# Deferred pieces of head norms are put in behind each filler step of an attention stage

## The reference

```python
h = rms_norm(x, g_mix)
proj = h @ w_in
qa, ka, va, qb, kb, vb, gate_a, gate_b = jnp.split(proj, cuts, axis=-1)
qa = rms_norm(qa.reshape(B, S, 16, 64), q_norm_swa)      # one norm per head of 64 columns
ka = rms_norm(ka.reshape(B, S, 2, 64), k_norm_swa)
qb = rms_norm(qb.reshape(B, S, 16, 64), q_norm_moba)
kb = rms_norm(kb.reshape(B, S, 16, 64), k_norm_moba)
y_a = swa_attention(qa, ka, va, sinks) @ w_up_swa        # window of 128 keys, 2 kv heads
y_b = moba_attention(qb, kb, vb) @ w_up_moba             # own block of 256, and 3 chosen past blocks
x = x + (sigmoid(gate_a) * y_a + sigmoid(gate_b) * y_b) @ w_out
x = x + hierarchical_moe(rms_norm(x, g_ffn), ...)
```

## Time and profile before

| | us |
|---|---|
| runs shown (median, lowest, highest) | 1942.26, 1939.7, 2071.72 (3 runs) |
| the profiled execution: its time | 1940.69 |
| the same: span of its slowest core (core 1) | 1939.1 |
| spans of the 8 cores | 1922.6 to 1939.1 |
| TensorE busy on core 1 | 1664.2 (86%) |
| ScalarE, VectorE busy | 743.0 (38%), 820.7 (42%) |

### The profile page before, as it was taken

The page is one execution under the profiler, slowest core; times in us unless marked ns, Lnnn a source line. Parts: engine busy times, 40 slices in busy tenths (PEclk is TensorE's granted clock), DMA queues, the critical chain, the costliest instruction groups (busy, mean ns, idle before and its releaser), DMA issues.

```text
span 1939.1 us, 30864 instructions; the slowest of 8 cores (1922.6 to 1939.1 us)
## 1 busy us (share of the span) xinstructions
PE 1664.2 (86%) x11342; PEld 1072.2 (55%) x11342; DVE 820.7 (42%) x1244; ACT 743.0 (38%) x1246; POOL 143.5 (7%) x283
## 2 busy tenths in 40 slices
PE   2775777889998988879999999998588899898995
PEld 1542344566566566454444444887466676666662
DVE  3634334434434443421211212233435567665765
ACT  4654446556665655671111110032331322323221
POOL 0010100200201200001111100000000000010000
PEclk9887888899999999989999999999789999999997
DMA  9469891895995999546998972851139789798796
GB/s 255 170 101 115 104 122 23 105 115 68 121 113 70 123 121 117 114 66 110 138 121 120 141 98 53 245 122 66 25 71 244 163 208 234 179 216 207 193 236 212
DMA packets 57084, 263.09 MB, mean 136 GB/s; under 512 B 10464, under 2 KB 10720, under 8 KB 49312
## 3 DMA queue, kind: packets, MB, share of 16 engines
q0 software_dynamic: 27168, 152.06, 57.7%
q1 hardware_dynamic: 29760, 108.96, 17.2%
HBM read 404.65 MB, written 73.40 MB: 247 GB/s over the span
## 4 chain that ended last, share of the span: by engine, by line
PE 72%; DVE 9%; ACT 7%; issue 5%; DMA 4%; SPq 1%; DVEq 0%; ACTq 0%
PE psum L1116 11%; PE psum L586 11%; PE psum L1529 10%; PE psum L607 6%; PE psum L1121 6%; PE psum L1304 6%; PE psum L1565 5%; PE psum L933 4%; PE psum L915 4%; DMA arena<-wbf 3%; PE psum L1551 3%; PE psum L1464 2%; DVE arena L1473 2%; DVE arena L921 1%; DVE arena L559 1%
## 5 line engine op out<-in xcount | busy, mean ns | idle before, releaser
L586 PE MATMUL psum<-arena 128*128 128x512 bf16 (+1 forms) x1072 | 286.7, 403 | 13.6 <-DVE arena L559 13.5
L1529 PE MATMUL psum<-arena 128*128 128x256 bf16 x2048 | 243.7, 273 | 5.8 <-DMA arena<-wbf 5.8
L1529 PEld LDWEIGHTS psum<-arena 128*128 128x128 bf16 x2048 | 199.8, 98 | 55.9 <-issue 8.3
L1116 PE MATMUL psum<-arena 128*128 128x512 bf16 x1024 | 226.2, 379 | 0.0
L926 ACT ACTIVATE arena<-psum 128x512 bf16<-128x512 f32 x352 | 197.9, 592 | 34.8 <-PE psum L915 33.3
L933 PE MATMUL psum<-arena 128*128 128x256 bf16 x832 | 164.6, 280 | 49.9 <-ACT arena L923 41.9
L586 PEld LDWEIGHTS psum<-arena 128*128 128x128 bf16 x1072 | 106.8, 103 | 121.1 <-issue 50.9
L1116 PEld LDWEIGHTS psum<-arena 128*128 128x128 bf16 x1024 | 100.2, 98 | 120.6
L915 PE MATMUL psum<-arena 78*128 78x256 bf16 x832 | 166.0, 281 | 0.0
L1554 DVE TENSOR_TENSOR arena<-psum,arena 128x1024 f32<-128x1024 f32 x128 | 153.8, 1221 | 10.2 <-PE psum L1551 4.0
L559 DVE SCALAR_TENSOR_TENSOR arena<-psum,arena 64x512 bf16<-64x512 f32 (+3 forms) x121 | 89.4, 739 | 144.1 <-ACT arena L556 136.6
(11 more groups left out here) (152 smaller groups left out, 1831.1 us busy)
## 6 DMA issues: line engine op xcount, KB each, us to landing
wbf<-wexp POOLq DMA_DIRECT2D x108, 512.0 KB, 36.1
arena<-wbf SPq DMA_DIRECT2D x108, 512.0 KB, 12.6
arena<-wexp POOLq DMA_DIRECT2D x84, 512.0 KB, 10.5
arena<-win POOLq DMA_DIRECT2D x58, 512.0 KB, 9.3
arena<-xs SPq DMA_DIRECT2D x24, 1024.0 KB, 8.3
arena<-wobf SPq DMA_DIRECT2D x14, 1024.0 KB, 6.0
wobf<-wo POOLq DMA_DIRECT2D x8, 1024.0 KB, 57.4
arena<-wup POOLq DMA_DIRECT2D x16, 512.0 KB, 11.8
```

The source lines that it names most:

```text
L586: prog.add("pe", lambda e, k=k: e.matmul(PS(bank, 0, n), lhsT=wslot[s][:, k, :], rhs=src[:, k, lo:lo + n], start=(k == 0), stop=(k == 15)) ...
L1116: prog.add("pe", lambda e, k=k, bank=bank, wt=wt, tl=tl: e.matmul(PS(bank), lhsT=wt[:, k, :], rhs=hTo[:, k, tl:tl + 512], start=(k == 0), ...
L1529: prog.add("pe", lambda e, k=k, f=f, bank=bank, Wv=Wv: e.matmul(PS(bank, f * 256, f * 256 + 256), lhsT=Wv[:, k, :], rhs=X[:, k, e4 * 256:( ...
```

## The change

`fill` now takes one piece out of `later` ahead of each filler step. Between two steps of four matmuls that follow each other there is thus one piece; the calls at the unit's end stay.

```diff
@@ -958,6 +958,7 @@
                 c, fns = steps[pos_[seg]]
                 pos_[seg] += 1
                 spent[seg] += c
+                pop_later()
                 for fn in fns:
                     fn()
```

## The result

The changed kernel takes 1895.21 us in the median of four runs (1892.64 to 1897.16). Against the kernel before, run beside it, the ratio is 0.9763, with a 95% interval of 0.9736 to 0.9791: faster by more than 2%, by some 46 us. A second set of six runs gave 0.9731.

The account below looks back on a forecast made before the run. TensorE bounds the block stage; the window stage loses time to TensorE's waits, chiefly for a PSUM bank. 28.9 - 4.3 + 13.5 + 4 - 5.5 = 36.6 us off 1940.7 gave 1904, forecast 1906 for the median; range 1889 to 1926.

Parts of the forecast that it names:

- The bank: Window stage: ten TensorE waits for L559's scaling, 28.3 us, go with their drains, less 1.0 for remains; gain 28.9 us.
- New waits of L550 in the window stage: Window stage: L550 follows its Square more closely at 18 places; loss 4.3 us, between 0 and 10.
- Ends of the groups: Window stage: last four units of a group, without filler, get shorter as norm pieces leave; gain 13.5 us, between 5 and 18.
- The clock: Window stage: slow matmuls behind four of the ten bank waits go, slow group starts stay; gain 4 us.
- The block stage: Block stage: L550 moved in 42 norms, its waits partly absorbed; loss 5.5 us, between -5 and 23.5.
- the groups repeat: Block stage: one group followed row by row, its net loss of 0.8 us applied to six groups, 0.7 in the seventh.
- The take-up by the diagonal tiles: Block stage: shorter waits at diagonal tiles absorb part of L550's delays, 0.4 and 0.2 us gained in the group followed.
- (a): Block stage: L550's waits are paid in full, 23.5 us instead of 5.5; time 1924, chance 0.15.
- (b): Window stage: TensorE keeps 2.4 GHz through the group starts also, 15 us more gain; time 1891, chance 0.14.
- (c): Window stage: ScalarE and VectorE take over, PV waits for them, 21 us less gain; time 1927, chance 0.08.
- (d): Window stage: last weight slice lands too late for the seventh group, costing some 10 us; time 1916, chance 0.03.
- (e): Block stage: logarithm delays a score exponential, 2.15 us for each of 42 norms; time 1990, slower, chance 0.03.

Follow-up runs that it names:

- window_only: Changed kernel, but pieces are taken out ahead of filler steps only in the window stage, block stage written as before: 1888.43 us, ratio 0.9723.
- block_only: Changed kernel, but pieces are taken out ahead of filler steps only in the block stage, window stage written as before: 1938.48 us, ratio 0.9973.
- early_second_only: Changed kernel, but each third piece in the block stage is held back to the unit where it stood before: 1900.92 us, ratio 0.9814.
- keep_warm: Changed kernel plus 192 small matmuls on constants in the last four units of window groups three to eight: 1888.76 us, ratio 0.9751.
- at_once: Changed kernel, but in the block stage the second piece directly follows its Square and the third goes in a unit earlier: 1954.54 us, ratio 1.0092.
- behind_matmuls: Changed kernel, but each piece is taken out behind a filler step's four matmuls instead of ahead, in both stages: 1893.54 us, ratio 0.9743.
- unit_end: Kernel before, but all waiting window-stage pieces go in at each unit's end: 1891.43 to 2081.45 us, no ratio; window stage 188.0 us.

## Why the prediction was right and where it was wrong

The time lies in the range, but it is faster by more than 2%, to which I had given 0.36. The forecast gain was 36.6 us, the measured one 46. The mechanism of the window stage was right. Two steps failed: that the groups of the block stage repeat, which put a loss of 5.5 us where there is none, and, in the clock's term, that the slow starts of the groups stay, which with what else was left out put 4 us where there are 11.3. By its terms, each from the same rows as the forecast's:

- **The bank, 28.9 forecast: right.** 28.3 us in ten waits and 1.6 of drains against 1.2 and 0.2: 28.5. window_only and block_only put the whole gain into this stage.
- **New waits of L550 in the window stage, −4.3: right.** 4.3 us in ten waits, 0.5 of which an old wait had, and 0.16 for each of eight more: −5.1.
- **Ends of the groups, 13.5: somewhat too high.** L765 4.0 less, L782 5.1 less (26.6 against 21.5), the gate L807 1.5 less: 10.6. L807 did not come down to the 0.6 of the block stage.
- **The clock, 4: mis-sized.** TensorE's busy time for the same matmuls fell by 11.3 us. Where they went can be read from the starts of the filler matmuls, which lie 0.216 us apart at full clock (0.108 with 256 columns): what a run of filler takes above this is the price of the lower clock. Behind the bank waits that was 5.0 us before and is nothing now; this is what I had counted, at 4. At the starts of the groups it was 16.4 us and is 13.1: 3.3 us that I had put at nothing, since the slow start "has its cause in the group's end and stays". The last 3 us lie in the value, score and norm matmuls (L782 alone 2.1). On the other cores the bank waits' part was 5.0 to 10.6 us. With 11.3 the four measured terms make 45.3 us, where the stage lost 45.1 on this core. That my sum for the stage, 42.1, is so near the 42.5 of the cores' mean is luck in part: three terms promised 4.1 us too much and the clock 7.3 too little.
- **The block stage, −5.5: wrong, and the step that failed is "the groups repeat".** For the middle groups the step held in its direction: 136.0 became 136.8, a loss of 0.4 us a group where I had 0.8. But the first group gained 2.4 us, and I had multiplied the middle group's loss into it as well. The windows of 10 us on TensorE, in the first group, from 30 us behind its start, of before and of the changed kernel (columns: us, PE busy, PEclk, DMA, GB/s) show what I had not followed:

```profile
381.30:391.30 10.00, 9.16 (x47) 0.83 0.99 105
```

```profile
330.80:340.80 10.00, 9.13 (x56) 1.00 1.00 109
```

Nine matmuls more go through in the same busy time. In the timeline of before a diagonal tile waits 2.39 us, and the four filler matmuls behind it take 1.58 us; in the changed kernel the wait is 1.52, and the next four take 1.02:

```profile
382.14 0.38 PE L933 MATMUL psum<-arena 128*128 128x256 bf16 x2 [2.39 <-ACT arena L923]
...
382.57 1.58 PE L586 MATMUL psum<-arena 128*128 128x512 bf16 x4
...
386.63 0.38 PE L933 MATMUL psum<-arena 128*128 128x256 bf16 x2
```

```profile
331.27 0.38 PE L933 MATMUL psum<-arena 128*128 128x256 bf16 x2 [1.52 <-ACT arena L923]
...
331.97 1.02 PE L586 MATMUL psum<-arena 128*128 128x512 bf16 x4
...
334.13 0.38 PE L933 MATMUL psum<-arena 128*128 128x256 bf16 x2
```

From this value matmul to the second one behind it, 4.49 us became 2.86. With the 0.87 us of shorter wait that is 2.5 us, the gain of the whole group. So a wait is shorter there, and the clock that had fallen behind the long one now holds. Core 0 of the kernel before has the same wait of 2.39 us, and 4.41 us behind it. block_only has the same 55.6 us without the change in the window stage. Neither piece does this alone: the third alone early gives 1.0 of the 2.4 us in this group, the second alone 0.9 (the table's first column). The clock is in both terms that were off, and both times I had undervalued it. (The upper bound of 23.5 us also counted 42 norms where by my own account 39 moved: 21.8.)

The take-up by the diagonal tiles was argued from one group, and the square of experiments bears it out: the waits of L550 are real (1.0 to 1.5 us a group are left of them), the third piece pays 0.6 to 1.1 back by being early itself, as the chain of the earlier trace rows said, and the rest of their 3.4 us a group is taken up whether it is early or not.

**The rivals.** (a), all L550 waits paid in full, is refuted by block_only, and its price by early_second_only: with L550 early and no third piece to pay for it the block stage is 9 us longer than before, not 23.5. (b), that the clock follows, lies nearest in time, 1891, but mostly not for its reason: of its 15 us, 3.3 came. The starts of the groups are still slow in the changed kernel, sixteen matmuls in 5.6 and 6.1 us, as in the earlier trace rows:

```profile
143.09 5.59 PE L586 MATMUL psum<-arena 128*128 128x512 bf16 x16
...
196.66 6.11 PE L586 MATMUL psum<-arena 128*128 128x512 bf16 x16
```

and keep_warm shows that more of what it spoke of could be had: its window stage is some 9 us shorter where nothing else was late. (c) did not come: L782 waits less for L772 than before. (d), to which I gave 0.03, did come, on three of eight cores, and I had its cause by halves. Counted from the start of the stage, which moved by 5.5 us itself, the load lands some 5 us earlier, as I had it, but the seventh group starts 40 us earlier where I had 31; that leaves 1.6 us of slack on core 1 and not 12. What it costs is 3 to 5 us on such a core, since the stage takes 190.7, 188.8 and 188.6 us on the three and 184.7 to 185.7 on three of the others; the last two, at 192.8 and 193.7, had a lower granted clock. On five cores this wait took back most of what keep_warm had gained in the stage. (e) did not come either, for the reason given against it, but its mechanism exists: at_once, which puts the logarithm behind the Square with no exponential between them (and the third piece a unit earlier), costs 1.5 us a norm where 2.15 was the price of the worst case.

What stays open: why behind_matmuls loses at both ends of the block stage and not in the middle. In its first group (core 5) the same value matmul waits 2.11 us, 0.6 more than in the changed kernel, and 4.56 us pass to the second one behind it, 1.7 more: 2.3 of the 2.8 us. For the 2.2 us at the other end, 1.8 of them between the marks of the sixth and seventh group, I have no such place. Open too are what the 2 us between unit_end's window stage and the changed kernel's are, and whether an earlier load of the last slice would let keep_warm keep its 9 us.

## What to carry to other kernels

When a stage's waits all name the operation that empties a buffer, look at where in program order that operation is written relative to the job that reuses the buffer: here a logarithm, an exponential and a scaling written ahead of some matmuls were worth 46 us with what followed from it, and how finely they were spread mattered by 2 us at most. Price a removed wait at its idle time and then ask at what clock the next matmuls run: with 34 us of idle time went 11 us of slow matmuls, 5 of them right behind the waits for a bank. And don't carry a per-group account to the first and last group without following them; a table of group lengths over all cores repeats within 0.1 us (the changed kernel's two sets), where the whole runs of one set lie 5 us apart.

## What the runs showed of the hardware

- A load that is issued 28 us earlier landed 10 us earlier: 71.2 us from issue to landing where it was 53.4. In both kernels ten conversions of other weights are issued on the same queue in the 6 us ahead of it, and in the window stage the mean busy share of the DMA engines rose from 0.77 to 0.97. That these are the cause is not shown.
- At one place of the block stage, four matmuls of 512 columns took 1.58 us behind a wait of 2.39 us (1.91 on core 0), 1.91 behind 2.11 us in behind_matmuls, and 1.02 behind 1.52 us. No rule follows: in the earlier trace rows four took 1.02 us behind a wait of 2.78 us, and the twelve after them 3.95.
- Small matmuls on constants, 192 more in the window stage, raised its granted clock from 0.87 to 0.93 and paid for themselves there: 9 us where nothing else was late.
- In at_once a matmul that waits for ScalarE and is waited for by ScalarE came with much more than its own wait: 0.84 us at L550 with 0.62 at L552 behind it, and 1.5 us a norm in the stage's length (third pieces moved too).
